# Order of work around the last attention pair, the first branch's GELU and the latent rotary step in a two-layer hybrid trunk

## What is computed

```python
(a_u, a_v, b_q, b_k, b_v, c_b, c_c, c_x,
 d_cq, d_ckv, d_kr, gate_logits) = split_columns(h @ w_in)
out_a = chunked_sgu(jax.nn.gelu(a_u), jax.nn.gelu(a_v), a_ln_g, a_ln_b, a_w_s, a_b_s)
out_b = moba_attention(rope(b_q), rope(b_k), b_v)          # 4 heads of 64
out_c = short_conv_mixer(c_b, c_c, c_x, c_w_conv)
out_d = mla_attention(d_cq, d_ckv, d_kr, ...)              # 4 heads, rotary part of 32
merged = sum_i sigmoid(gate_i) * (branches[i] @ w_branch[i])
x = x + rms_norm(merged @ w_out, g_post_mix)
x = x + rms_norm(square(relu(rms_norm(x) @ w_mlp_in)) @ w_mlp_out, g_post_mlp)
```

## Time and profile before

| | us |
|---|---|
| median of 3 runs (lowest, highest) | 803.23 (801.64, 805.15) |
| the profiled execution, device time | 803.02 |
| its span in the profile | 801.2 |
| PE busy | 780.7 |
| DVE, ACT, POOL busy | 554.7, 410.5, 62.5 |

### The profile page before, as it was taken

The page is one execution under the profiler, slowest core; times in us unless marked ns, Lnnn a source line. Parts: engine busy times, 40 slices in busy tenths (PEclk is TensorE's granted clock), DMA queues, the critical chain, the costliest instruction groups (busy, mean ns, idle before and its releaser), DMA issues.

```text
span 801.2 us, 11018 instructions
## 1 busy us (share of the span) xinstructions
PE 780.7 (97%) x3989; PEld 656.5 (82%) x3989; DVE 554.7 (69%) x826; ACT 410.5 (51%) x643; POOL 62.5 (8%) x86
## 2 busy tenths in 40 slices
PE   9999899979999999999999999999799999999997
PEld 6898688868888888888889977888688888888885
DVE  5689686778777565655666986766887765655663
ACT  7555655533465444444546655565236654444441
POOL 1210000006120000000020100000142000000000
PEclk9999999999999999999999999999999999999999
DMA  9685655543467555666826755655444676666641
GB/s 315 183 266 165 205 179 168 181 157 106 133 205 239 185 184 186 184 204 213 276 66 203 247 182 158 188 171 167 136 134 152 190 231 189 183 204 187 183 128 53
DMA packets 88201, 145.87 MB, mean 182 GB/s; under 512 B 10316, under 2 KB 51556, under 8 KB 88164
## 3 DMA queue, kind: packets, MB, share of 16 engines
q1 hardware_dynamic: 88020, 145.24, 58.2%
q10 hardware_dynamic: 144, 0.13, 0.0%
HBM read 144.31 MB, written 1.05 MB: 181 GB/s over the span
## 4 chain that ended last, share of the span: by engine, by line
PE 82%; DVE 11%; ACT 3%; DMA 2%; issue 1%; POOL 1%; POOLq 0%; SPq 0%; DVEq 0%
PE banks L1405 20%; PE banks L1407 19%; PE banks L1406 19%; PE banks L1453 11%; PE banks L1454 5%; DVE w_lo L867 5%; DVE qkTB L1002 2%; PE banks L1457 2%; DMA raw<-in_w_in_dram 1%; PE banks L1508 1%; DVE probsT L989 1%; PE banks L1615 1%; PE banks L1456 1%; ACT w_hi L531 1%; PE banks L1417 1%
## 5 line engine op out<-in xcount | busy, mean ns | idle before, releaser
L867 DVE TENSOR_TENSOR w_lo<-raw,w_hi 128x1024 fp32r<-128x1024 f32 (+1 forms) x256 | 303.8, 1217 | 107.9 <-ACT w_hi L531 107.7
L531 ACT CAST w_hi<-raw 128x1024 fp32r<-128x1024 f32 (+1 forms) x256 | 256.9, 1040 | 112.2 <-PE banks L1457 45.9
L1405 PE MATMUL banks<-w_hi,xT_both 128*128 128x512 f32 (+2 forms) x472 | 182.3, 386 | 4.5 <-ACT gate_th L597 4.5
L1407 PE MATMUL banks<-w_hi,xT_both 128*128 128x512 f32 (+2 forms) x472 | 179.0, 379 | 0.0
L1406 PE MATMUL banks<-w_lo,xT_both 128*128 128x512 f32 (+2 forms) x472 | 178.9, 379 | 0.0
L1453 PE MATMUL banks<-xT_both,w_hi 128*128 128x512 f32 x364 | 130.4, 397 | 0.0
L1405 PE MATMUL banks<-w_hi,brT_hi 128*128 128x512 f32 x320 | 126.9, 396 | 0.0
L1407 PE MATMUL banks<-w_hi,brT_lo 128*128 128x512 f32 x320 | 125.6, 392 | 0.0
L1406 PE MATMUL banks<-w_lo,brT_hi 128*128 128x512 f32 x320 | 125.5, 392 | 0.0
L1405 PEld LDWEIGHTS banks<-w_hi,xT_both 128*128 128x128 f32 x472 | 89.1, 189 | 24.6 <-ACT gate_th L597 6.1
L1407 PEld LDWEIGHTS banks<-w_hi,xT_both 128*128 128x128 f32 x472 | 89.0, 189 | 16.5
(11 more groups left out here) (197 smaller groups left out, 758.0 us busy)
## 6 DMA issues: line engine op xcount, KB each, us to landing
raw<-in_w_in_dram SPq DMA_DIRECT2D x88, 512.0 KB, 4.5
raw<-in_w_mlp_in_dram SPq DMA_DIRECT2D x64, 512.0 KB, 4.7
raw<-in_w_mlp_out_dram SPq DMA_DIRECT2D x64, 512.0 KB, 4.3
raw<-in_w_branch_dram SPq DMA_DIRECT2D x16, 512.0 KB, 4.0
raw<-in_w_out_dram SPq DMA_DIRECT2D x16, 512.0 KB, 3.6
gate_th<-in_w_in_dram SPq DMA_DIRECT2D x8, 512.0 KB, 8.2
raw<-in_w_in_dram SPq DMA_DIRECT2D x8, 352.0 KB, 6.2
x<-in_x_dram SPq DMA_DIRECT2D x4, 256.0 KB, 4.3
```

Of the source, the lines that this page charges most:

```text
L531: nc.scalar.copy(w_hi[:, c % RING, h * n:(h + 1) * n], raw_of(q)[:, 0:n]).then_inc(hi_ready, 1)
L867: v.tensor_tensor(w_lo[:, c % RING, cut], raw_of(q)[:, 0:n], w_hi[:, c % RING, cut].bitcast(F32), ALU.subtract).then_inc(lo_ready, 1)
L1405: nc.tensor.matmul(dst, l_hi, r_hi, start=first, stop=False)
L1407: return nc.tensor.matmul(dst, l_lo, r_hi, start=False, stop=last)
```

## The change

Three things are moved; nothing is added or taken away.

- The values of head pair 3 stand behind unit 7 instead of unit 3 on PE. On ACT the rounding of branch D's result (`branch_hi(l, 3)`) and its wait stand behind the casts of chunk 32 instead of ahead of them. On DVE `branch_lo(l, 3)` stands behind `gate_unit(7)` instead of `gate_unit(3)`.
- The GELU of `a_u`: DVE's polynomial moves from s = 12 to s = 15, ACT's tanh from s = 13 to s = 16 and DVE's last step from s = 13 to s = 16. ACT's square stays at s = 12.
- The latent rotary embedding on DVE moves from s = 12 to s = 13, that is behind the split of chunk 15.

```diff
-        LAST_VALUES_AFTER = 3
+        LAST_VALUES_AFTER = 7
...
-                if s == 13:
+                if s == 16:
                     act.wait_ge(u_inner, nth(l, 1, 0))
                     nc.scalar.activation(u_tmp, u_tmp, ACT.Tanh, scale=GELU_SCALE).then_inc(u_tanh, 1)
...
+                split(l, C_OUT)
                 act.wait_ge(attn_psum, nth(l, 4, 3))
                 branch_hi(l, 3, psum[:, 2, :])
-                split(l, C_OUT)
                 split(l, C_OUT + 1)
...
-                if s == 12:
+                if s == 13:
 
                     dve.wait_ge(q_rope_copied, nth(l, 1, 0))
                     h, o = D_ROPE // 2, B_ROT
...
                     v.tensor_tensor(k_rope[:, :, h:D_ROPE], tmp[2], tmp[3], ALU.add).then_inc(ropeD_ready, 1)
+                if s == 15:
                     dve.wait_ge(u_squared, nth(l, 1, 0))
                     v.tensor_scalar(u2, u_tmp, GELU_CUBE, 1.0, ALU.mult, ALU.add).then_inc(u_poly, 1)
                     dve.wait_ge(u_poly, nth(l, 1, 0))
                     v.tensor_tensor(u_tmp, u2, psum[:, 3, :], ALU.mult).then_inc(u_inner, 1)
-                if s == 13:
+                if s == 16:
                     dve.wait_ge(u_tanh, nth(l, 1, 0))
                     v.scalar_tensor_tensor(u2, u_tmp, 1.0, psum[:, 3, :], ALU.add, ALU.mult).then_inc(u_gelu, 1)
...
                 gate_unit(l, 2)
                 gate_unit(l, 3)
-                branch_lo(l, 3, ORDER_D, psum[:, 2, :])
                 split_half(l, C_OUT, 0)
                 gate_unit(l, 4)
                 split_half(l, C_OUT, 1)
                 for n in range(5, 8):
                     gate_unit(l, n)
+                branch_lo(l, 3, ORDER_D, psum[:, 2, :])
                 split_half(l, C_OUT + 1, 0)
```

## The result

The changed kernel takes 792.88 us (median of 6 runs, 791.65 to 793.71) against 803.30 us of the kernel before in the same comparison: a ratio of 0.9869, 95% interval 0.985 to 0.9887, so 1.3% or 10.4 us faster. The profiled execution took 792.57 us, 790.8 in its span; that of the kernel before 803.02 and 801.2. The forecast was 791.4 us, the range 788.4 to 797.0.

What follows compares the result with a forecast made beforehand. PE was taken as the bound, busy 780.7 of 801.2 us, so only its waits and slow stretches could be won. 4.7 + 7.5 - 0.6 = 11.6 us off 803.02 gave 791.4 us, range 788.4 to 797.0.

Steps and rivals of the forecast that it cites:

- part A: Steps 12 to 16, the GELU and rotary moves: 1.55 us gained in the first layer, 3.15 in the second, 4.7 in sum.
- part B: Units behind pair 3's moved values: 4.35 us gained in the first layer, 3.15 in the second, 7.5 before 0.6 lost behind.
- masks 1.7 us earlier: VectorE ahead of pair 0's masks: they start 1.7 us earlier, so PE loses 0.55 instead of 2.25 us at chunk 14.
- 0.15 us more at chunk 16: Moved GELU work at steps 15 and 16 adds 0.15 us to the 0.27 us PE waits there.
- 1.60 us for the second layer's half clock: Behind the second layer's chunk 14 wait: the shorter wait removes the slow stretch, worth 1.60 us.
- The rotary embedding costs and gives nothing: VectorE's rotary move behind one split stays ahead of the masks: no effect on them.
- the schedule of units 4 to 15: From unit 3's end to the first output product, 20.75 us in each layer, 7.5 us gained in both.
- 0.3 us a layer behind it, for chunk 34: GpSimd's last two additions meet VectorE's split of chunk 34: 0.3 us lost in each layer, 0.6 in all.
- Half clock among the units: Rival: PE's idling at gates 0 to 2 keeps the clock low, adding 2.4 us: 793.8 us; chance 0.27.
- A wait handed on: Rival: a meeting with GpSimd delays branch_lo and unit 10 by up to 1.3 us: 794.0 us; chance 0.09.
- Part B does nothing: Rival: the idle time returns whole at units 5 to 10, part A alone stands: 798.9 us; chance 0.05.
- VectorE bound through the port and slower than before: Rival: eight VectorE passes each wait for a GpSimd addition, 9.7 us a layer: 810.8 us; chance 0.03.

Runs made afterwards that it cites:

- e6: Changed kernel with GpSimd's eight additions a layer cut from 512 to 8 columns: 791.30 us, ratio 0.9853 to the kernel before.
- e7: Changed kernel with five of pair 3's transposes moved from ahead of gate 0 to behind gate 3: 793.30 us, ratio 0.9877 to the kernel before.
- e4: Kernel before with only the rotary embedding moved behind the split of chunk 15: 803.00 us, ratio 0.9989.
- e5: Kernel before with 38 identity transposes keeping PE busy in the wait ahead of pair 3's values: 799.04 us, ratio 0.9952.
- e1: Kernel before with only the last pair's values, with their rounding and low part, moved behind unit 7: 796.91 us, ratio 0.9927.
- e2: Kernel before with only the GELU and the rotary embedding moved: 799.30 us, ratio 0.9954.
- e3: Kernel before with only the GELU moved, the rotary embedding left where it was: 798.58 us, ratio 0.9953.
- e9: Changed kernel with pair 0's masks ahead of branch C's low part and GELU's tanh behind rotary copies and gate tanh: 791.72 us, ratio 0.9866 to the kernel before.
- e10: Changed kernel unaltered, run again in the same rounds as e9: 793.04 us, ratio 0.9887 to the kernel before.
- e8: Changed kernel with VectorE's low part of branch D put back behind gate 3, values still behind unit 7: 802.09 us, ratio 0.9993 to the kernel before.

## Why the prediction was right, and where it was off

The sum was 11.6 us, measured are 10.4. In the profiles part A gained what was forecast (4.67 beside 4.7 us), part B 5.86 instead of 6.9. Step by step:

**Part A, masks 1.7 us earlier.** Right in kind, 1.4 us in the first layer: from chunk 14's start to its second tile 84.08 - 80.53 = 3.55 us instead of 4.99. Of the missing 0.3 us, 0.2 are what the prediction's lower bound was made of: the cast of chunk 16 waited 1.10 us for its transfer, and the split behind it took 2.56 us for two halves instead of 2.36.

```profile
78.50 1.05 ACT L531 CAST w_hi<-raw 128x1024 fp32r<-128x1024 f32 x1 [1.10 <-DMA raw<-in_w_in_dram]
```

The wait at chunk 14 was under 0.6 us in both layers of this profile, as forecast (0.52 us and none). In other profiles with the same part A it reached 0.86 us (e6, e7).

**0.15 us more at chunk 16.** Right: from 84.08 to 96.17 it takes 12.09 us instead of 11.94.

**1.60 us for the second layer's half clock.** Right in these two profiles, where A gained 3.40 us there against 3.15 forecast, and wrong as a property of the second layer. There are seven waits of 1.76 to 2.16 us at chunk 14: two each in before, e4 and e5, and the one in e1's first layer (e1's other one is 0.93 us and is left out). Half clock followed twice, in before's second layer and in e4's first. By these seven the term is a chance of 2 in 7 in each layer, about 0.9 us in all. That part A came out right for the profiles was luck: the profile of the kernel before happened to hold that stretch once. In the medians part A is worth 3.7 (e2) to 4.4 us (e3).

**The rotary embedding costs and gives nothing.** Right (e4).

**Part B, the schedule of units 4 to 15.** From unit 3's end to the first output product 20.75 us were worked out; 192.97 - 172.08 = 20.89 were measured in the first layer and 581.16 - 560.27 = 20.89 in the second (172.08 and 560.27 are the starts of unit 4 less their waits of 1.30). The waits at gates 1 and 2 show 0.15 and 0.23 us instead of 0.5 and 0.45, but cost about that much. The trace counts idle time from the shown end of the last product, 0.16 us (0.39 - 0.23) after the next was due, and the first product behind a wait is followed after 0.34 instead of 0.23 us:

```profile
175.16 0.50 PE L1406 MATMUL banks<-w_hi,brT_hi 128*128 128x512 f32 x1 [0.15 <-DVE rows L1150]
175.50 0.39 PE L1407 MATMUL banks<-w_lo,brT_hi 128*128 128x512 f32 x1
```

That makes 0.27 us more than shown. `branch_lo`, with 0.15 us to spare in the forecast, ended at 182.86 and didn't hold unit 10, which started at 183.70.

That the total agrees to 0.14 us is closer than its parts. GpSimd's six additions took 10.46 us instead of the 9.65 worked out, as three of them were slow (2.21 to 2.31 us) and not two, and the 0.5 us added for meetings covered that: the first half of the way back ended 20.74 us after unit 3, as forecast (192.14 + 0.68 - 172.08). But by the forecast PE would have been there at 20.25 us and waited. It did not wait: its own work took it to 20.89 us, as the units took 0.4 us more than worked out and the transposes with unit 15 took 2.47 instead of 2.25 us. That the two paths met at the same time was in part luck.

**0.3 us a layer behind it, for chunk 34.** This is the mis-sized term, and one of the prediction's own signs of being wrong, chunk 34 coming late, did appear, with 0.26 us shown. From the first output product to the second merged transposes it takes 8.87 and 8.82 us instead of 8.19 and 8.17, 0.7 us a layer. The mechanism was the named one, VectorE's pass of chunk 34 against GpSimd's last additions: 2.01 us instead of 1.22. But the price was set between nothing and one addition instead of adding up all meetings in a stretch where VectorE has hardly any idle time. In the changed kernel these are 0.5 us in chunk 33's second half, 1.0 in the two additions for tile 0, 0.8 in chunk 34's first half, and 0.7 us of idling for GpSimd's sum, 3.0 us in all. e6, without them, gives back only 0.9 us a layer, because VectorE then idles elsewhere, for the merged rows that PE and ScalarE bring back:

```profile
194.08 1.29 DVE L1165 SCALAR_TENSOR_TENSOR xT_both<-banks,xT_both 128x512 fp32r<-128x512 f32 x2 [1.74 <-ACT xT_both L603]
```

**The rivals.** Half clock among the units: didn't happen in any of the profiles e1, e6, e7, e9, e10 and the changed kernel, whose B all lie within 0.1 us (e6's 0.9 lower). The six timed executions of the changed kernel, too, have a mean granted clock of 0.998 or 0.999. A wait handed on: only 0.7 us at chunk 34. Part B does nothing: refuted by e1. VectorE bound through the port and slower than before: the mechanism is there, at 0.9 us a layer, a tenth of its price.

The Trainium skill's rule on the shared port (SBUF — State Buffer, section Who interferes with whom), that whoever issues first holds it for a whole instruction, is borne out by the two meetings whose ends can be read. In the changed kernel GpSimd is first, and the half split of chunk 34 ends 1.1 us after the addition, as above. In e6 VectorE is first: GpSimd's addition of 8 columns, which takes 0.20 us alone, starts 0.16 us behind a split, takes 1.12 us and ends 0.06 us after it.

```profile
181.57 1.22 DVE L867 TENSOR_TENSOR w_lo<-raw,w_hi 128x1024 fp32r<-128x1024 f32 x1
181.73 1.12 POOL L1395 TENSOR_TENSOR rows<-rows,gate_th 128x8 f32<-128x8 f32 x1 [129.02 <-DVE gate_th L1150]
```

## What to carry to other kernels

A wait of the busiest engine can cost more than its length: where the clock fell behind it, a quarter to four fifths of it came on top here (1.1 us behind 4.25 us in e5's comparison, 1.6 behind 1.95). So look at the product spacing or the granted clock behind the wait before you price its removal, and read two executions before you call a clock stretch a property of a place. When a move lets one engine run ahead, sum up the work of the engine that serves it between two of its landmarks, with all passes that meet another engine's at their lengthened duration; where that sum fills the stretch, expect little from further reordering (e7 gained nothing) and count each idle microsecond of that engine in full (e8). Follow also the chain that its passes start on a third engine: here GpSimd's additions behind gate 4. A step that is moved on one engine must be moved on those that wait for it: left behind, `branch_lo` alone took back 9 of the 10 us.

## What the runs showed of the hardware that was not expected

- The same wait of 1.95 us was followed by 1.2 GHz in one layer and by 2.4 GHz in the other, and in two profiles it was not the same layer. The stretches behind it were granted 1.00 of full speed in the first layer and 0.57 in the second in the kernel before, and 0.72 and 1.00 in e4. The wait of 3.23 us in e8 had the drop behind it in the second layer (0.72) and none in the first. All eight waits of 4.25 us (before, e2, e3, e4) had it, at a price that varied: B from 61.30 to 62.72 us, where e5 with a busy PE has 60.3. What decides stays open.
- Transposes of the identity held the clock: with 38 of them in each of the two waits, 4.31 us long in the first layer, it stayed at 1.00 in the profiled execution, and the median fell by 4.0 us.
- In e8's second layer the clock fell to 0.72 from 577 to 583 us, yet B is as long as in the first layer, 63.53 and 63.57 us: the half clock cost nothing here, where PE was not the bound.
